# A 192-byte shift of every buffer behind the weight ring in a two-block transformer kernel

## The reference

```
x = x + ab_mixer(h, ...)          # mLSTM and stick-breaking attention, layer 0
x = x + c_mixer(h, ...)           # gated delta net, layer 1
x = x + mem_cross_attn(rmsnorm(x, xa_norm[l]), memn, wq, wk, wv, wo)
x = x + sq_relu_mlp(rmsnorm(x, mlp_norm[l]), w1, w2)      # d_ff 4096
# second block: FoX and DSA attention (layer 0), MoBA attention (layer 1), then
x = x + conv_glu_ffn(rmsnorm_2(x, ...), w_up, conv_w, conv_b, w_down)   # d_ff 2816
```

## Time and profile before

| | |
|---|---|
| median of 3 runs | 1635.77 us |
| the profiled execution | 1636.0 us, span 1634.2 us |
| TensorE matmul busy | 1561.1 us (96%), 12614 records |
| GpSimd busy | 1192.3 us (73%) |
| ScalarE, VectorE busy | 830.4 us (51%), 759.9 us (46%) |
| mean granted TensorE clock | 0.979 |

### The profile page before, as it was taken

How to read it: one execution, slowest core, us unless ns; L and a number is a source line. 1 busy time by engine, 2 the same in 40 slices (tenths; PEclk the granted TensorE clock), 3 DMA queues, 4 the chain that set the end, 5 groups by cost and what they waited for, 6 DMA issues and landing times. The chain is left out here.

```text
span 1634.2 us, 32576 instructions
## 1 busy us (share of the span) xinstructions
PE 1561.1 (96%) x12614; PEld 1491.0 (91%) x12614; DVE 759.9 (46%) x1385; ACT 830.4 (51%) x1250; POOL 1192.3 (73%) x920
## 2 busy tenths in 40 slices
PE   7989999999999798999999999889999999999997
PEld 6978989999998688998999998779999997899997
DVE  5554644220187656534422016945554128465522
ACT  4663555554465553555555445355545443554542
POOL 5655967999977500596799896706999987189995
PEclk9999999999999998999999999979999999899999
DMA  6433535555554200353555553405656553155663
GB/s 264 143 103 104 193 117 168 194 194 194 191 166 148 90 1 1 115 194 105 178 195 194 193 182 130 142 1 171 195 194 194 194 189 129 40 180 193 194 195 104
DMA packets 67662, 248.04 MB, mean 152 GB/s; under 512 B 7632, under 2 KB 7888, under 8 KB 67152
## 3 DMA queue, kind: packets, MB, share of 16 engines
q1 hardware_dynamic: 67536, 246.19, 45.4%
HBM read 245.11 MB, written 1.05 MB: 151 GB/s over the span
## 5 line engine op out<-in xcount | busy, mean ns | idle before, releaser
L345 POOL TENSOR_TENSOR ring_lo<-ring,ring_hi 128x512 fp32r<-128x512 f32 x916 | 1192.1, 1341 | 424.1 <-ACT ring_hi L999 421.9
L999 ACT ACTIVATE ring_hi<-ring 128x1024 fp32r<-128x1024 f32 x458 | 465.9, 1052 | 202.0 <-DMA ring<-panels 193.6
L379 PE MATMUL ps_dve<-x_hi,ring_hi 128*128 128x256 f32 x1928 | 461.0, 280 | 17.8 <-POOL ring_lo L345 11.1
L379 PE MATMUL ps_dve<-x_lo,ring_hi 128*128 128x256 f32 x1928 | 456.4, 278 | 0.0
L379 PEld LDWEIGHTS ps_dve<-x_hi,ring_hi 128*128 128x128 f32 x1928 | 364.1, 189 | 24.1 <-issue 15.6
L379 PEld LDWEIGHTS ps_dve<-x_lo,ring_hi 128*128 128x128 f32 x1928 | 364.1, 189 | 0.5 <-issue 0.2
L379 PE MATMUL ps_dve<-x_hi,ring_lo 128*128 128x256 f32 x1928 | 271.4, 278 | 0.1
L379 PEld LDWEIGHTS ps_dve<-x_hi,ring_lo 128*128 128x128 f32 x1928 | 243.6, 188 | 0.9 <-POOL ring_lo L345 0.7
L379 PE MATMUL ps_dve<-work_parts,ring_hi 128*128 128x256 f32 x1728 | 225.3, 276 | 0.0
L379 PEld LDWEIGHTS ps_dve<-work_parts,ring_hi 128*128 128x128 f32 x1728 | 211.7, 188 | 0.0
L1488 DVE TENSOR_TENSOR xT<-xT,ps_dve 128x512 f32<-128x512 f32 x40 | 27.5, 688 | 312.3 <-PE ps_dve L379 312.1
(11 more groups left out here) (285 smaller groups left out, 1997.6 us busy)
## 6 DMA issues: line engine op xcount, KB each, us to landing
ring<-panels SPq DMA_DIRECT2D x458, 512.0 KB, 3.5
consts<-constants SPq DMA_DIRECT2D x1, 1700.0 KB, 11.7
xT<-x_t SPq DMA_DIRECT2D x1, 1024.0 KB, 5.3
scratch<-mem_t SPq DMA_DIRECT2D x1, 1024.0 KB, 17.7
out_t<-xT SPq DMA_DIRECT2D x4, 256.0 KB, 2.2
smalls<-small_operands SPq DMA_DIRECT2D x1, 824.5 KB, 14.5
consts<-constants SPq DMA_DIRECT2D x1, 129.5 KB, 5.2
angle_i<-positions SPq DMA_DIRECT2D x1, 128.0 KB, 8.1
```

The lines of the kernel that those rows point to most:

```text
L345: pool.tensor_tensor(ring_lo[:, s, cs], ring[:, s, cs], plain(ring_hi[:, s, cs]), ALU.subtract).then_inc(sem("lo_made"), 1)
L379: ins = pe.matmul(o, lhsT, rhs, start=start, stop=stop, skip_group_check=True)
L999: tell(act.activation(ring_hi[:, n % RING, :], ring[:, n % RING, :], ACT.Copy), "hi_made")
```

## The change

The unused buffer ahead of `xT` shrinks from 88 to 40 floats a partition, from 352 to 160 bytes. Every buffer behind it begins 192 bytes earlier: `xT` at 87424, `x_hi` at 95616, `work` at 152960. The activation buffers are then 384 modulo 512, which is 256 from the ring's 128, in `project` and in `project_tokens` alike. The ring, `consts` and `smalls` stay where they are. No instruction is added, removed or moved on any engine.

```
         consts = sb("consts", [P, N_CONST])
         smalls = sb("smalls", [P, N_SMALL])
-        sb("stream_margin", [P, 88])
+        sb("stream_margin", [P, 40])
         xT = sb("xT", [P, C, T])
```

## The result

The changed kernel takes 1687.27 us, the median of 5 runs (1678.66 to 1689.7). The ratio to the kernel before is 1.0308 (95% interval 1.0269 to 1.0347): 3% slower, 51.5 us between the medians, where I had forecast 12 us. The profiled execution is the fastest of the five, 1678.66 us with a span of 1676.9 us. Two further executions of the kernel before are on record, 1633.22 us and a single one of 7256.57 us, four times any other, which is left out.

The account below looks back on a forecast made before the run. TensorE was taken to bound the kernel, by matmul count times pitch. The profiled 1636.0 us plus 12.6 us for 2790 matmuls going to the long pitch, other engines and DMAs at 0, gave 1648.6, stated as 1648; range 1612 to 1676.

Parts of the forecast that it names:

- What bounds the kernel: Whole kernel: TensorE, busy 1561.1 of 1634.2 us with short waits; time is the number of matmuls times their pitch.
- The change part by part, item 3: Ring matmuls' pitch at full clock: 2790 matmuls change from 113.3 to 117.8 ns, 12.6 us; loss bounded by 39.4 us.
- The last paragraph's alternative: Sign in ring matmul stretches: a pitch neither 113.3 nor 117.8 means distance acts on each matmul, 10.7 us per ns.
- The restarts: Ring matmul stretches: distance decides whether a restart finds the short pitch; more than now go wrong at 256.
- the 14 of 14 of `project_tokens`: Trace before: all 14 restarts of `project_tokens` (distance 64) end at the long pitch, beside 17 of 50 in `project`.
- The rival of no change: Ring matmuls: distance has nothing to do with the pitch; 1636 us, within 3 us; chance 0.27.
- Faster: Ring matmuls: at 256 each restart finds the short pitch, 1627.4 us, or 1610 with a lower pitch; chance 0.28.
- Slower, to the end: Ring matmuls: every restart falls into the long pitch and none comes back, plus 39.4 us, 1675.4; chance 0.18.
- The floor: Ring matmuls at full clock: streaming alone 106.7 ns; pitches are 6.6 or 11.1 over, from weight hand-over or interfering reads.

Follow-up runs that it names:

- the mirrored kernel: Kernel before with `stream_margin` of 120 floats: distance 64 in `project` and 448 in `project_tokens`, the mirror of before; 1656.26 us, ratio 1.0102.

## Why the prediction was wrong

- *What bounds the kernel* was right: TensorE by pitch alone. (One reading of the rows is rough: (1.10 - 0.281) / 7 is 117 ns and not 118; a timeline of two digits can't tell them apart, and the windows give 117.9.) The other engines kept their work, no wait appeared, and a gain or loss in the pitch went to the end without cover.
- *The change part by part, item 3, is the step that failed*, in both its halves. First, I took the two known pitches as the only ones, with 117.8 as "the longest pitch that any row has" and the bound of the loss at 39.4 us. The change brought a third, 120.0. Second, I placed 256 between 448 and 64 by its distance modulo 512 and let a part of the restarts change over: 2790 matmuls, 12.6 us. The period is 256 bytes, so that 256 is a distance of 0, and I had no row of that. Every matmul paid: 8760 x 6.7 + 1920 x 2.2 = 62.9 us, against 64.3 measured, where I had 12.6. The bounds were not bounds, since nothing in the trace said that rows at two distances cover a third.
- *The last paragraph's alternative* was the right reading, and I gave no chance to it with a longer pitch than the two: a stretch "neither 113.3 nor 117.8" means that the distance acts on each matmul, at 10.7 us a ns. The mean step went from 114.17 to 119.95 ns, 5.8 x 10.7 = 62 us.
- *The restarts.* That the 14 of 14 of `project_tokens` were due to its distance and not to its form is borne out by the mirrored kernel, where it finds the short pitch in 8 of 14. (At the old distance with both buffers moved it was 1 of 14, so the 14 of 14 is no law.) The symmetry that made me hesitate (equal pitches at 448 and 64) is only that both pitches exist at both; how often each is found differs much.
- *The rival of no change*, with the Trainium skill's rule behind it, is refuted by the two kernels that move only the reads. *Faster*, on the thought that half a block keeps the reads apart, is wrong for the same reason as my own step: half of 512 is a whole period. The argument that I set against it, that the start only moves the meeting of the two reads in time, fails too: the starts alone move the pitch by up to 6.7 ns. *Slower, to the end* had the direction and three quarters of the size (39.4 of 51.5 us), by the wrong pitch.
- *The floor*: 6.6 ns over the 106.7 of the streaming stay at the best place. No distance took any of it, and at half the clock none of the ten costs anything: in each trace the steps of the ring's matmuls there have a median of 213 ns. What the 6.6 are is open.
- *What I left out* is the scatter of single executions. The clock alone, 0.981 to 0.992 over the five runs of the changed kernel, is worth 8 to 11 us, and the kernel before spreads by 21 us at one and the same clock. Both belong in the range, but neither made the forecast wrong.

Open remain the reason for 256 bytes, and what decides at 448 and 192 whether a restart finds 113.3 or 117.8, or at 384 and 416 which level a stretch takes.

## What to carry to other kernels

Where a stream of matmuls bounds a kernel, read the distance from start to start and not the durations, and compare it between stages of the same form: two values there are a sign that something besides the instructions sets it. Then the start addresses of the moving and the stationary operand are worth a sweep, since an unused buffer of some hundred bytes is all it takes; sweep a whole period before reasoning about where the best place is, and take several executions of each, since one place can show two pitches. And a bound taken from the trace holds for what the trace contains: if a parameter takes a value that no row has, the range has to allow for a level that no row has.

## What the runs showed of the hardware

- With 256 float columns moving and 128 float columns loaded for the next matmul, the pitch at the full clock depends on the distance of the two start addresses modulo 256 bytes: 113.3 or 117.8 ns at 192 (and 448), 117.8 nearly always at 64 (and 320), a mean of 118.7 in nearly all long stretches at 128 (and 384, whose first held 120.0), 120.0 at 0 (and 256).
- At one and the same distance, 448, the stream held 113.3 ns for 1532 matmuls and, behind an added one, 117.8 ns for 983. In the kernel before, what a stretch holds is settled within the first few steps after a restart in all but one case; a 64-column matmul in between moved it from the short to the long pitch in 19 of 19 cases.
- At the half clock the pitch is 213 ns at distances 448 and 256 alike, and in the traces of the other eight.
